# Stores on ScalarE's queue and earlier state products in a one-core hybrid decoder layer

## The reference, cut to what matters

```python
mod = silu(c) @ w_ada + b_ada                       # shifts, scales and gates: 1024 x 6144
h = rmsnorm(x, g_pre_mix) * (1 + sc_mix) + sh_mix
proj = h @ w_in                                     # 1024 x 3340: pool input, q/k/v, z, a, b
pool_out = pool_mixer(...)                          # causal means over 2, 4, 8, 16
q, k, v = silu(causal_conv(...))                    # then l2 norms of q and k
# gated delta rule: tinv = inverse of (I + strictly lower L) per chunk and head,
#   v_new = u - w @ s ; o = q_dec @ s + qk @ v_new ; s = s * decay + k_dec^T @ v_new
# prompt: the state starts at zero; samples: state_ssm (8, 6, 128, 128) is read, updated, written
mix = concat(pool_out, norm(o) * silu(z)) @ w_out
x = x + gt_mix * rmsnorm(mix, g_post_mix)
h = rmsnorm(x, g_pre_ffn) * (1 + sc_ffn) + sh_ffn
f = top-4-of-32 experts: ((up + 1) * glu(gate)) @ w_down[e]   # w_gu 32 x 1024 x 2048, w_down 32 x 1024 x 1024
x = x + gt_ffn * rmsnorm(f, g_post_ffn)
```

## Time and profile before

| | |
|---|---|
| median of 3 runs (lowest, highest) | 1237.64 us (1234.45, 1238.09) |
| profiled execution: own time / span | 1234.33 us / 1232.4 us |
| mean granted TensorE clock | 0.953 |
| PE, PEld, VectorE, ScalarE, GpSimd busy | 89%, 45%, 21%, 19%, 20% |
| HBM read / written | 455.54 MB / 7.57 MB, mean 376 GB/s over the span |
| chain that ended last | PE 66%, DMA 17%, SP's queue 8%, VectorE 5% |

### The profile page before, as it was taken

One profiled execution on the slowest core, in us unless ns is written; L12 is line 12 of the kernel. 1 busy time (PEld: TensorE's weight loads), 2 busy tenths in 40 slices (PEclk: granted clock), 3 DMA queues, 4 the chain that ended last, 5 costly groups with the idle time before them and its releaser, 6 DMA issues.

```text
span 1232.4 us, 30076 instructions
## 1 busy us (share of the span) xinstructions
PE 1093.1 (89%) x12069; PEld 559.7 (45%) x12070; DVE 262.1 (21%) x748; ACT 232.8 (19%) x566; POOL 245.9 (20%) x515
## 2 busy tenths in 40 slices
PE   4899979999999769999789999999666699999995
PEld 4678757556444324444234444444222244444442
DVE  1045683864011101111011111111000011111112
ACT  2241313142111101111011111111000011111112
POOL 0041103202222212222112222222201112222220
PEclk9999999987999989999789999999878899999998
DMA  9946937798999999999999938999999999999997
GB/s 339 333 145 232 339 96 215 289 359 346 428 427 428 428 429 428 428 429 429 428 430 428 428 152 341 429 428 428 430 427 429 430 427 429 429 428 430 428 428 296
DMA packets 77253, 463.64 MB, mean 376 GB/s; under 512 B 11339, under 2 KB 30481, under 8 KB 52570
## 3 DMA queue, kind: packets, MB, share of 16 engines
q1 hardware_dynamic: 69903, 460.86, 91.0%
q10 hardware_dynamic: 7315, 2.27, 0.9%
HBM read 455.54 MB, written 7.57 MB: 376 GB/s over the span
## 4 chain that ended last, share of the span: by engine, by line
PE 66%; DMA 17%; SPq 8%; DVE 5%; issue 2%; ACT 1%; ACTq 0%; DVEq 0%
PE psum L641 24%; PE psum L668 13%; DMA work<-in_w_down 7%; PE psum L595 5%; SPq L882 4%; PE psum L990 4%; DMA weights<-in_w_gu 4%; DMA weights<-in_w_down 4%; PE psum L617 4%; PE psum L651 2%; PE psum L1241 2%; SPq L885 2%; DMA weights<-in_w_ada 2%; PE psum L606 1%; PE psum L613 1%
## 5 line engine op out<-in xcount | busy, mean ns | idle before, releaser
L641 PE MATMUL psum<-weights,work 128*32 128x512 f32 x2928 | 351.6, 628 | 63.7 <-DMA weights<-in_w_gu 55.7
L2492 POOL TENSOR_SCALAR work<-work 128x128 f32<-128x128 f32 x159 | 123.8, 789 | 609.7 <-PE psum L659 609.7
L641 PEld LDWEIGHTS psum<-weights,work 128*32 128x32 f32 x2928 | 95.5, 113 | 300.1 <-issue 211.6
L2332 DVE TENSOR_TENSOR work<-psum,work 128x256 f32<-128x256 f32 x53 | 22.5, 425 | 811.1 <-PE psum L651 811.1
L668 PE MATMUL psum<-weights,work 128*32 128x256 f32 x2624 | 153.1, 381 | 3.2 <-DMA weights<-in_w_down 3.2
L1766 ACT COPY work<-psum 128x512 f32<-128x512 f32 x53 | 31.0, 585 | 467.7 <-PE psum L641 467.7
L668 PEld LDWEIGHTS psum<-weights,work 128*32 128x32 f32 x2624 | 79.5, 110 | 60.2 <-DVE work L2341 8.9
L595 PE MATMUL psum<-work 128*32 128x256 f32 (+1 forms) x1296 | 90.5, 394 | 0.6 <-ACT work L1721 0.6
L990 PE MATMUL psum<-work,weights 128*128 128x288 f32 x320 | 81.0, 410 | 0.0
L641 PE MATMUL psum<-work 128*32 128x512 f32 x464 | 57.1, 611 | 22.8 <-issue 11.6
L595 PEld LDWEIGHTS psum<-work 128*32 128x32 f32 (+1 forms) x1296 | 38.0, 111 | 69.0 <-issue 59.8
(11 more groups left out here) (400 smaller groups left out, 972.7 us busy)
## 6 DMA issues: line engine op xcount, KB each, us to landing
weights<-in_w_gu SPq DMA_DIRECT2D x112, 2048.0 KB, 32.5
weights<-in_w_down SPq DMA_DIRECT2D x48, 2048.0 KB, 36.2
work<-in_w_gu SPq DMA_DIRECT2D x16, 2048.0 KB, 27.1
work<-in_w_down SPq DMA_DIRECT2D x16, 2048.0 KB, 39.1
weights<-in_w_ada SPq DMA_DIRECT2D x12, 2048.0 KB, 12.8
weights<-in_w_in SPq DMA_DIRECT2D x6, 2048.0 KB, 14.1
weights<-in_w_out SPq DMA_DIRECT2D x2, 2048.0 KB, 8.5
out<-weights SPq DMA_DIRECT2D x8, 512.0 KB, 7.0
```

Of the source, the lines that this page charges most:

```text
L641: last = mm(bank(GB)[SLOTS * n:SLOTS * n + SLOTS, :], xTm[:, k % 2, k // 2, :], gu[:, k % 2, 512 * n:512 * n + 512], start=k == 0, stop=k ...
L2492: ins = g.tensor_scalar(selG[:, c, :], iota_bd if c == 2 else iota, cur[:, 0, c:c + 1], cur[:, 1, c:c + 1], ALU.is_equal, ALU.mult)
```

## The change

The diff below leaves out addresses of small router tiles, the moves on GpSimd (three small memsets) and lines that only follow from these.

- **Front.** SP saves the gate rows and reads them back (`modG`, `gate_rows`) before it stores the solved blocks, not after. On PE and ACT each level of the inverse stands one unit later: levels 1 and 2 after unit 24, 3 and 4 after unit 25. `sample_reads(0)` stands ahead of `new_values(1, 2)`.
- **Middle.** All stores of states and of x after the mixer are issued by ACT, between its own operations. `state_update(2, 0)` and `(2, 1)` stand before the last `mix_half`, the second in banks 0 and 1, and VectorE applies them before `add_mix(2)`.
- **Loads.** (1,2) now stands before (1,0), (1,4) before (1,3) and waits for `x1` 3; (1,5) waits for the transposed bias rows (`setup_ps` 5). These transposes stand before `back(0, 6)`, not after the last `back`.
- **End.** The samples' rows are finished and stored before the prompt's.

```diff
@@ state_bank (new)
+        def state_bank(i, m):
+            return 0 if 2 * i + m == H - 1 else 2
@@ SP
+            sp.wait_ge(s["modG"], 4)
+            for j in range(4):
+                sp.dma_start(gm_dram[:, :, P * j:P * j + P], modG[32 * j:32 * j + SEQS]).then_inc(s["modG_st"], 16)
+                sp.dma_start(gs_dram[...], modG[...]).then_inc(s["modG_st"], 16)
+            sp.wait_ge(s["modG_st"], 128)
+            gate_rows(sp, 0, gm_tok, "gm_in")
             sp.wait_ge(s["pooled"], 2)
             sp.wait_ge(s["t0"], 2)
             sp.dma_start(t_dram...).then_inc(s["blk"], 16)
             t_block_loads(sp, 0)
-            (the same gate stores, wait and gate_rows stood here)
...
             sp.wait_ge(s["o_ps"], 2)
             load(0, 2)
-            sp.wait_ge(s["sp_new"], 1)
-            sp.dma_start(ssm_prompt[0, 0]...).then_inc(s["ssm_out"], 16)
...
-            store_states(0)
-            store_x1(0)
-            store_x1(1)
             sp.wait_ge(s["mix_ps"], 3)
             load(0, 5)
-            store_states(1)
+            sp.wait_ge(s["ssm_out"], 16 * 5)
+            load(1, 2)
             sp.wait_ge(s["mix_ps"], 4)
             load(1, 0)
-            sp.wait_ge(s["ssm_out"], 16 * 5)
-            load(1, 2)
-            store_x1(2)
-            store_states(2)
             sp.dma_start(bgu_rows, ...).then_inc(s["rb_in"], 16)      # and four of b_down
+            sp.wait_ge(s["x1"], 3)
+            load(1, 4)
             sp.wait_ge(s["ssm_out"], 16 * (1 + H))
             load(1, 3)
             sp.wait_ge(s["x2T_ps"], 5)
             sp.wait_ge(s["ssq"], 9)
             load(1, 1)
-            load(1, 4)
             sp.wait_ge(s["x1_st"], 48)
-            sp.wait_ge(s["rank_done"], 1)
-            sp.wait_ge(s["gate_done"], 2)
-            sp.wait_ge(s["router_ps"], 6)
+            sp.wait_ge(s["setup_ps"], 5)
             load(1, 5)
...
-            for c in range(2):
-                sp.wait_ge(s["fin_y"], c + 2)
-                sp.dma_start(y_prompt...)
-            sp.wait_ge(s["fin_y"], 4)
+            sp.wait_ge(s["fin_y"], 2)
             for q in range(NQ):
                 sp.dma_start(y_sample...)
+            for c in range(2):
+                sp.wait_ge(s["fin_y"], c + 3)
+                sp.dma_start(y_prompt...)
@@ PE, after_unit and after the units
                 if u == 23:
                     pe.wait_ge(s["qkdT"], 3)
-                    pe.wait_ge(s["blk"], 16 * BLK_LOADED)
-                    level_product(pe, mm, 1)
-                    level_product(pe, mm, 2)
                     pe.wait_ge(s["silu_done"], CT)
                     to_tokens(3, PB)
                     conv_tails()
+                if u == 24:
+                    pe.wait_ge(s["blk"], 16 * BLK_LOADED)
+                    level_product(pe, mm, 1)
+                    level_product(pe, mm, 2)
+                    pe.wait_ge(s["kv_tok"], 4)
+                    to_tokens(4, PB)
+                    last_tails()
                     level_updates(pe, mm, 1)
                     level_updates(pe, mm, 2)
...
+            pe.wait_ge(s["ssm_in"], 16 * NSEQ)
             pe.wait_ge(s["tu_done"], last_step(1))
+            sample_reads(0)
             pe.wait_ge(s["kv_tok"], 6)
             new_values(1, 2)
-            pe.wait_ge(s["ssm_in"], 16 * NSEQ)
-            sample_reads(0)
...
             state_update(1, 1)
+            state_update(2, 0)
+            pe.wait_ge(s["ssq"], 5)
+            state_update(2, 1)
             mix_half(1, 4, 1).then_inc(s["mix_ps"], 1)
             transposes_x2(0, 6)
-            state_update(2, 0)
+            pe.wait_ge(s["s_new"], 2 * H)
             transposes_x2(1, 1)
             logits(0, 6)
             logits(1, 1)
             transposes_x2(2, 4)
-            state_update(2, 1)
+            pe.wait_ge(s["rb_in"], 16 * 5)
+            (transposes of the bias rows into bank 3, counts setup_ps 5)
             pe.wait_ge(s["lg_sb"], 1)
             back(0, 6)
@@ ACT
             output_root(1)
+            act.wait_ge(s["sp_new"], 1)
+            act.dma_start(ssm_prompt[0, 0]...).then_inc(s["ssm_out"], 16)
             output_root(2)
...
             mix_root(0)
+            act.wait_ge(s["ssm_out"], 16)
+            store_states(0)
             mix_root(1)
+            store_x1(0)
             x1_root(0)
             x1_root(1)
+            store_x1(1)
             act.wait_ge(s["modT"], 4)
             mix_root(2)        # with store_states(1) between its two halves
             modulate_prompt(0, 6)
+            act.wait_ge(s["ssm_out"], 16 * 5)
+            store_states(2)
             x1_root(2)
+            store_x1(2)
@@ VectorE
             for t in range(2):
                 new_states(1, 1, t)
+            for m in range(2):
+                for t in range(2):
+                    new_states(2, m, t)
             add_mix(2)
-            for t in range(2):
-                new_states(2, 0, t)
             normed(2)
```

More of the change, by code:

```diff
@@ L1371, in _ @@
             transposes_x2(2, 4)
-            state_update(2, 1)
+            pe.wait_ge(s["rb_in"], 16 * 5)
+            pe.wait_ge(s["s_new"], 2 * H - 2)
+            for q in range(4):
+                last = tr(bank(3)[:, P * q:P * q + P], bgu_rows.rearrange("p (n j) -> p j n", j=4)[:, q, :], ident)
+            last.then_inc(s["setup_ps"], 1)
             pe.wait_ge(s["lg_sb"], 1)
@@ L2246, in _ @@
                    ALU.mult, ALU.add).then_inc(s["h2T_v"], 1)
-            for t in range(2):
-                new_states(2, 1, t)
             top_experts(2, 1)
```

117 lines of the change are left out of this document (51 added, 66 removed).

## The result

Sixteen runs of the changed kernel have their median at 1239.15 us (1235.85 to 1242.6), sixteen of the kernel before at 1235.32 us. The ratio is 1.0029, with a 95% interval of 1.0019 to 1.0039: 3.6 us slower, where 7.1 us faster was forecast. (The three runs that the forecast started from had their median 2.3 us above that of the sixteen.) The profiled execution of after took 1239.35 us with a span of 1237.4, 5.0 us longer than that of before.

What follows compares the result with a forecast made beforehand. The prediction took the weight-load stream to bound the kernel until 640 us, then TensorE. Refills 6.3 us earlier (1.2 by TensorE, 5 by the debt) plus 0.8 at the end made 7.1: 1237.6 to 1230.5 us, range 1223.5 to 1239.

Steps and rivals of the forecast that it cites:

- What bounds the kernel: Expert loop: weight loads set the pace from 300 to 640 us, TensorE from 700; time won early stays to the end.
- Front, "gains 5.3 us": Units 23 to 25 up to the state products: these begin at 203.5 instead of 208.81 us, 5.3 us won (2 to 7).
- my estimates from these rows at full clock: Front behind unit 24: products, tokens, tails 2.2 us, updates 1.0, unit 25 2.0, products and tokens 2.4, updates 1.6.
- Last half, "+4.4 us": Last projection half: waiting for VectorE's update and two early state update pairs start it at 262.8 instead of 258.35 us.
- rival (d): Before the last half TensorE's clock falls; 9 to 12 us lost, first expert at 306 to 309, 1239.7 to 1242.7 us; chance 0.12.
- Given back and bias rows, -0.3 us with ACT's 0.2: Last half to first expert: 1.3 us given back, bias-row wait costs 0.8 (0 to 3), ScalarE's stores 0.2.
- Debt 5 us to 0: First refill: 5 us of the first twelve loads still owed before, none after; refills start at 300.7 instead of 307.
- End 0.8 us: Kernel end: samples' rows stored while VectorE scales the prompt's rows, 0.8 us won (-0.5 to 2).
- Stores on ScalarE worth nothing in bandwidth: Moving stores to ScalarE's queue gains no bandwidth, as all issuers share 16 DMA engines; the sum takes none.

Runs made afterwards that it cites:

- e8: The kernel before with the change's front and end, state loads held until the level 1 and 2 updates, state products and outputs ahead of sample reads; ratio 0.9975.
- e4: The kernel before with the change's front alone; ratio 1.0007 (0.9996 to 1.0019).
- e11: The changed kernel with e8's hold of the state loads and e8's place of the first sample reads; ratio 0.9999 to the kernel before.
- e2: The changed kernel with its front back in the order of before; ratio 1.0024 to the kernel before, median 1238.79 us.
- e13: The changed kernel with ScalarE's store of x1(2) ahead of its last two state stores instead of behind them; ratio 1.0025 to the kernel before.
- e6: The kernel before with the change's end alone, samples normed and stored ahead of the prompt's rows; ratio 0.9992.
- e5: The changed kernel with front, group 2 state updates, bias transposes and load (1,4) as before; ratio 0.9997 to the kernel before.
- e3b: The changed kernel with group 2 state updates, bias transposes and load (1,4) in their old places; ratio 1.0014 to the kernel before.
- e1: The changed kernel with only the three stores of x1 issued by SyncE again; ratio 1.0020 to the kernel before.
- e10: e8 without the hold of the eight state loads, issued where the change issues them; ratio 1.0008 to the kernel before.
- e7: The kernel before with the change's front, state loads held until the level 3 updates, new values ahead of sample reads; ratio 1.0047.
- e9: e8 with the state loads held one level later, until the updates of level 3; ratio 1.0015 to the kernel before.
- e12: e8 with TensorE's state reads ahead of the first two sample reads; ratio 0.9951 to the kernel before, six runs counted.
- e14: The same kernel as e12, run once more; ratio 0.9941 to the kernel before.

## Why the prediction was wrong, step by step

- **What bounds the kernel: right as far as it was tried.** A first expert 12.4 us later cost 7.0 at R and 5.0 in the span, the new end included.
- **Front, "gains 5.3 us": the step that failed first.** It cost 3.3 us in P (40.0 for 36.7). The blocks, the cover by unit 24 and the landing of the states were sized well enough: e8 reached 31.7, the forecast being 31.4. What failed is "my estimates from these rows at full clock" and, ahead of it, that the state loads go out at 186 for nothing. I gave the eight loads a landing time, but did not ask what runs beside them: TensorE's densest stretch of small matmuls. Before, they were issued from 192.68, behind that stretch, and ran beside the rest of unit 24 and small matmuls that came a third as fast. Of the 8.6 us between forecast and trace, the stop of 2.96 us and the half clock for the 10 us behind it make 7.5. About 1.3 more are unit 24, priced at 7.03 us behind a gap of 2 us, although I had noted half clock behind the gap of 6.02 myself. In time the lost front is +0.9 us by e4, not clear of zero; that its gain was there to be had is shown by e11, 3.7 us faster than after with e8's front.
- **Last half, "+4.4 us": mis-sized, by the mechanism of rival (d).** The wait was right (2.33 us here), the clock wrong. From P to the end of the half it took 64.3 us instead of 56.7, 7.6 more: the wait, 3.78 for the pairs and 1.48 for the half. The five kernels with the early updates have pairs of 2.8 to 3.8 us and a half of 8.5 to 9.7; in all others the half takes 7.13. Rival (d) gave the pairs 4.2 us, the half up to 6.0 more, and a first expert at 306 to 309 (310.39). That it comes so near the measured start is partly luck: it kept the front's gain of 5.3 us and overpriced the half. It had a chance of 0.12, too little: the row with 2.08 us a pair stood in front of me.
- **Given back and bias rows, -0.3 us with ACT's 0.2: wrong in this trace, by the clock.** From the end of the half to the first expert it took 35.1 us instead of 32.5. (The terms listed as given back add up to 1.6, not 1.3.) ScalarE, 0.2 us in my sum, stood for 8.84; it was priced by the state stores' issue time on SyncE, not by what an x store behind them takes (4.69 us before). But that hold did not lengthen the stretch: e2 and e11 have it too and took 31.8 us, near the forecast, at a higher clock, and e13, without it, took 34.6. What decides the clock there stays open.
- **Debt 5 us to 0: right.** From the first expert to R it took 172.4 us, before 177.8: 5.4 us given back, so that a start 12.4 us later is 7.0 at R.
- **End 0.8 us: right,** 1.0 by e6 (0.9992, with an interval that still holds 1) and 1.1 by the spans of e2 and before.
- **Stores on ScalarE worth nothing in bandwidth: right.** e5 less e6 is +0.6 us, within the error. The rule of the Trainium skill that I drew on there (Trainium Kernel Development and Optimization, Key Constraints: several issuers share the 16 DMA engines and only save issue time) agrees with that.

In ratios the parts add up to the change: front +0.0007 (e4; by undoing it +0.0005, after less e2, or +0.0017, e3b less e5), early updates +0.0015 to +0.0027 (e3b against after, e5 against e2), end -0.0008 (e6) and the rest +0.0005 (e5 less e6). With e4's front that is 0.0019 to 0.0031, measured 0.0029. Each of these differences is uncertain by 0.001 or more, so only the early updates stand clear of zero, and that the sum comes out is no proof of its other parts. Not settled: how much each of the wait, the half clock and the late bias rows contributes to the middle, and what decides on which side of a stretch the clock falls.

The Trainium skill (TensorE: Matmul & The Clock Gate, Part 1) has activity release the throttle. These rows don't bear that out for TensorE's busy time: it was busy for 5.00 of 5 us from 198 to 203 at 0.50.

## What to carry to other kernels

When a block of transfers in small packets moves, look at what the engines execute beside it, not only at when it lands: where the trace shows an engine stopped at issue, hold the transfers behind the dense small instructions, and put work that doesn't need it in front of the wait. Price an issue by what stands ahead of it on the same queue; a large store behind small-packet stores held the whole engine here. Look at the granted clock of a stretch before you give its length to anything else. And a term that rests on "at full clock" needs a second figure at half clock and a chance that fits the nearest slow row.

## What the runs showed of the hardware

- TensorE stopped for 2.65 to 3.01 us at issue, with no semaphore awaited, in after, e1, e3b, e4, e10 and e13, whose state loads (8 of 384 KB) ran beside some 200 small matmuls, and for 0.24 to 0.64 us in e7, e8, e9, e12 and e14, with the loads held. Hold and no hold differ by one wait in e8 and e10, so that the loads bring the stop is shown.
- TensorE went on 2.2 to 2.8 us behind the start of a packet of instructions (0.02 MB, queue q8) in all 14 such stops of the front. The packets come over the DMA engines that the loads fill: their share was 1.07 to 1.20 around the stop in after.
- Half clock set in within 1.3 us of the end of each of the six stops of over 2.6 us in the front, and lasted through stretches in which TensorE was busy throughout. Behind e8's stop of 1.25 us it did not set in.
- A DMA issue on ScalarE took 0.35 or 8.84 us for the same store (e13, after), by whether state stores had just been issued ahead of it on its queue.
- With the early updates the way from the last half to the first expert took 29.8 us at a granted clock of 0.77 (e1), 31.8 at 0.73 (e2, e11) and 34.6 and 35.1 at 0.60 and 0.61 (e13, after).
